# Experts as jobs of 256, 320 or 416 rows, with upper products of seven half-size products, on one Trainium2 core

## The reference

```python
def moe_swiglu(t, w_router, w1, w3, w2):
    logits = (t @ w_router).astype(jnp.float32)
    top_v, top_i = lax.top_k(logits, TOP_K)
    gates = jax.nn.softmax(top_v, axis=-1).astype(t.dtype)
    e_flat = top_i.reshape(-1)
    order = jnp.argsort(e_flat)
    tok = order // TOP_K
    xs = t[tok]
    sizes = jnp.bincount(e_flat, length=N_EXPERTS).astype(jnp.int32)
    h = jax.nn.silu(lax.ragged_dot(xs, w1, sizes)) * lax.ragged_dot(xs, w3, sizes)
    y = lax.ragged_dot(h, w2, sizes) * gates.reshape(-1)[order][:, None]
    return jnp.zeros_like(t).at[tok].add(y)
```

## Time and profile before

| | us |
|---|---|
| median of 3 runs | 9414.39 (9413.78 to 9432.35) |
| the profiled execution | 9423.43 |
| its span, first to last instruction | 9421.8 |
| TensorE busy | 8953.0 (95%) |
| VectorE busy | 2786.4 (30%) |
| ScalarE busy | 1255.4 (13%) |
| GpSimd (POOL) busy | 810.0 (9%) |

### The profile page before, as it was taken

How to read it: one execution, slowest core, us unless ns; L and a number is a source line. 1 busy time by engine, 2 the same in 40 slices (tenths; PEclk the granted TensorE clock), 3 DMA queues, 4 the chain that set the end, 5 groups by cost and what they waited for, 6 DMA issues and landing times. The chain is left out here.

```text
span 9421.8 us, 116793 instructions
## 1 busy us (share of the span) xinstructions
PE 8953.0 (95%) x45206; PEld 6543.9 (69%) x45207; DVE 2786.4 (30%) x5410; ACT 1255.4 (13%) x3193; POOL 810.0 (9%) x856
## 2 busy tenths in 40 slices
PE   9975999999999999889999999999999999999995
PEld 4454566557777767348777788777788777787774
DVE  2346455333343443541211211111111111111113
ACT  1134222220011110220000100000100000100002
POOL 0010000013343422010000000000000000000002
PEclk9986999999999999989999999999999999999997
DMA  5312000135555522233311211122211221211235
GB/s 223 134 48 88 12 6 6 71 132 198 190 209 194 207 86 83 84 135 107 115 67 67 92 42 53 53 93 80 91 67 67 76 71 67 92 53 67 89 107 196
DMA packets 498755, 922.04 MB, mean 98 GB/s; under 512 B 31404, under 2 KB 357084, under 8 KB 491632
## 3 DMA queue, kind: packets, MB, share of 16 engines
q1 hardware_dynamic: 426310, 667.60, 20.8%
q0 software_dynamic: 64320, 222.87, 6.1%
q10 hardware_dynamic: 7920, 28.84, 1.0%
HBM read 685.85 MB, written 231.23 MB: 97 GB/s over the span
## 5 line engine op out<-in xcount | busy, mean ns | idle before, releaser
L2610 PEld LDWEIGHTS ex_psH<-ex_xt,ex_w 128*128 128x128 f32 x23296 | 3331.9, 192 | 183.3 <-issue 183.3
L2610 PE MATMUL ex_psH<-ex_xt,ex_w 128*128 x23296 | 3385.6, 306 | 21.1 <-issue 18.1
L2620 PE MATMUL ex_psY<-ex_w,ex_a 128*128 128x512 f32 x2912 | 1309.9, 592 | 0.8 <-DVE ex_a L2769 0.8
L2769 DVE TENSOR_TENSOR ex_a<-ex_s,ex_psH 128x128 f32<-128x128 f32 (+1 forms) x728 | 237.3, 326 | 2958.3 <-ACT ex_s L2715 2958.3
L2620 PEld LDWEIGHTS ex_psY<-ex_w,ex_a 128*128 128x128 f32 x2912 | 535.3, 190 | 523.6 <-issue 520.6
L2776 DVE TENSOR_TENSOR ex_ya<-ex_psY,ex_ya 128x512 f32 (+2 forms) x676 | 571.5, 845 | 1046.5 <-PE ex_psY L2620 842.6
L2715 ACT ACTIVATE ex_s<-ex_psH 128x128 f32<-128x128 f32 (+1 forms) x728 | 224.2, 308 | 4532.0 <-PE ex_psH L2610 4531.9
L694 PE MATMUL de_ps<-de_w,de_big 128*128 128x512 f32 x1408 | 618.1, 596 | 24.8 <-DVE de_big L911 24.8
L694 PEld LDWEIGHTS de_ps<-de_w,de_big 128*128 128x128 f32 x1408 | 267.5, 191 | 350.1 <-issue 307.1
L259 PE MATMUL en_psO<-en_w,en_ht 128*128 128x512 f32 (+4 forms) x1152 | 473.4, 571 | 2.0 <-ACT en_ht L301 2.0
L2591 POOL DMA_DIRECT2D ys<-ex_ya x16 | 9.2, 573 | 5055.0 <-issue 5055.0
(11 more groups left out here) (387 smaller groups left out, 7054.2 us busy)
## 6 DMA issues: line engine op xcount, KB each, us to landing
ex_w<-in_o_w SPq DMA_DIRECT2D x336, 1024.0 KB, 7.7
de_wr<-in_e_w SPq DMA_DIRECT2D x88, 1024.0 KB, 5.3
xs<-de_zero POOLq DMA_DIRECT2D x130, 512.0 KB, 4.6
ys<-de_zero POOLq DMA_DIRECT2D x130, 512.0 KB, 5.4
en_ch<-in_w_mod SPq DMA_DIRECT2D x48, 1024.0 KB, 5.3
de_w<-in_e_w SPq DMA_DIRECT2D x44, 1024.0 KB, 5.1
ex_x<-xs ACTq DMA_DIRECT2D x55, 512.0 KB, 3.6
proj<-en_o POOLq DMA_DIRECT2D x18, 1008.0 KB, 4.2
```

Source lines behind the costliest of these rows:

```text
L2610: last = nc.tensor.matmul(psH[:, h, q * width:(q + 1) * width], W[:, s, k, h * P:(h + 1) * P], XT[:, k, bass.ds(at, width)], start=k == 0, ...
L2620: last = nc.tensor.matmul(psY[:, c], A[:, h, 0:P], W2[:, s, h, c * BANK:(c + 1) * BANK], start=h == 0, stop=h == HU - 1)
L2769: nc.vector.tensor_tensor(A[:, h, 0:width], S[:, h, 0:width], psH[:, h, width:2 * width], ALU.mult).then_inc(a_done, 1)
```

## The change

An expert is now cut into jobs of 2h rows, h being 128, 160 or 208. A table made on the host, `job_table`, gives for each number of 32-row units the cheapest set of jobs; on chip, VectorE picks for each expert the row of the table by its count, orders the jobs by size (all of 256 rows first, then 320, then 416) and writes a list with each job's first row, its expert and its half size. `experts` loops over the jobs of each size. The job is the outer loop now, and the chunks of 256 hidden columns the inner one, so every job streams its expert's 44 MB of weights again. YA holds one job and is double buffered; the stores to `ys` have moved from POOL to SyncE's queue. The upper products go by seven half-size products, `up` in the diff. Every job turns four tiles of 128 rows, for the next job, in its last two chunks (the `hooks`), and VectorE makes its four token sums (832 elements each) behind the last chunk's sums. The upper products are accumulated in PSUM banks 0 to 3, the down products in 4 to 6, and bank 7 takes the transposes. In `fourier` the old planning goes and the list's making comes in its place; `xs` and `ys` are six tiles of 128 rows longer.

```diff
+HALVES = (128, 160, 208)
+PS = m.psum("ps", [P, 8, BANK])
...
+def job_table():
+    sizes = [2 * h // UNIT for h in HALVES]
+    best = [(0.0,) + (0,) * NS]
+    for u in range(1, LEVELS):
+        options = []
+        for t, n in enumerate(sizes):
+            cost, *jobs = best[max(0, u - n)]
+            jobs[t] += 1
+            if sum(j * k for j, k in zip(jobs, sizes)) < LEVELS:
+                options.append((cost + n * UNIT + 6,) + tuple(jobs))
+        best.append(min(options))
+    return np.array([b[1:] for b in best], np.float32).T
...
 (fourier, VectorE: the list)
+            for e in range(NE):
+                last = nc.vector.scalar_tensor_tensor(PT[:, e], RI[:, 0:TABLE], U[:, e:e + 1], RI[:, TABLE:2 * TABLE], ALU.is_equal, ALU.mult)
+            settle(last)
+            settle(nc.vector.reduce_sum(SEG[:, :, 0:NE].rearrange("a t e -> a e t"), PT.rearrange("a e (t u) -> a e t u", t=NS), AXX))
...
+            for k in range(SEGS):
+                last = nc.vector.tensor_scalar(VQ[:, :, k], JOT, PRE[:, k:k + 1], DIF[:, k:k + 1], ALU.is_ge, ALU.mult)
+            settle(last)
+            settle(nc.vector.reduce_sum(JF[:, 0], VQ, AXX))
...
 (experts, SyncE: within a job)
+                    with sp.Fori(1, FC // 2) as q:
+                        for s in range(2):
+                            f = sp.snap((q * 2 + s).with_bounds(min_val=2, max_val=FC - 1))
+                            used(f - 2, 0)
+                            sp.dma_start(W1[:, s], pick(w1v, e, f)).then_inc(w1_in[s], 16)
+                            used(f - 2, 1)
+                            sp.dma_start(W3[:, s], pick(w3v, e, f)).then_inc(w3_in[s], 16)
+                            used(f - 2, 2)
+                            sp.dma_start(W2[:, s], pick(w2v, e, f)).then_inc(w2_in[s], 16)
...
 (TensorE)
+                        pe.wait_ge(comb["c22"], u + 1)
+                        product("p1", w, quarter(W, s, 0, 0), tokens(0, 0))
+                        pe.wait_ge(comb["c21"], u + 1)
+                        pe.wait_ge(sums["s2"], u + 1)
+                        pe.wait_ge(t_made, j + 1)
+                        product("p6", 2, SM[:, w, 1], token_sum(1))
+                        pe.wait_ge(comb["c12"], u + 1)
+                        product("p7", 3, SM[:, w, 0], token_sum(2))
+                        if hooks:
+                            half_turn(hooks[2 * w], j + 1)
+                        pe.wait_ge(comb["u2"], u + 1)
+                        product("p4", 2, quarter(W, s, 1, 1), token_sum(3))
+                        pe.wait_ge(kept, u + 1)
+                        product("p2", w, quarter(W, s, 0, 1), tokens(1, 0), start=False)
...
+                        product("p5", 1 - w, quarter(W, s, 1, 0), token_sum(0))
+                        if hooks:
+                            half_turn(hooks[2 * w + 1], j + 1)
+                        pe.wait_ge(comb["u3"], u + 1)
+                        pe.wait_ge(sums["s4"], u + 1)
+                        product("p3", 3, SM[:, w, 2], tokens(1, 1))
...
 (TensorE, down products: part o in bank 4 + o % 3)
+                            if o < 3:
+                                pe.wait_ge(y_added[t], first + 1)
+                            else:
+                                pe.wait_ge(y_added[t], first + (o - 1))
...
 (VectorE, a chunk)
+                        for w in range(2):
+                            combine(g, w, hooks)
+                        if hooks and hooks[-1] == 2 * TILES - 1:
+                            token_sums(dve.snap((j + 1).with_bounds(min_val=1, max_val=JOBS)), other)
...
+                        for o, (cols_n, r0, rows_n, c0, width, place) in enumerate(parts):
+                            dve.wait_ge(y_done[t], done + (o + 1))
+                            out, new = YA[:, bass.ds(y0 + place, width)], PS[:, 4 + o % 3, 0:width]
```

More of the change, by code:

```diff
@@ L2535, in plan @@
[L2535 to L2547, removed]
+        YA = m.sbuf("ya", [P, 2 * YW])
@@ L2563, in used @@
[L2563 to L2566, removed]
[L2568 to L2579 removed]
+            w1v = w1.rearrange("e (k p) (f n) -> e f p k n", p=P, n=FW)
@@ L2603, in _ @@
+            n, ahead = sized(pool, len(HALVES) - 1)
+            with pool.Fori(0, (n + ahead) * (FC // 2)) as q:
+                for s in range(2):
+                    for w in range(2):
+                        weight_sums(q * 4 + (2 * s + w), s, w, q)
         @block.tensor
         def _(pe):
+            pe.sem_inc(prod["p3"], 2)
             pe.wait_ge(const_in, 32)
-            def up(s, h, at, width):
-                for q, W in enumerate((W1, W3)):
-                    for k in range(KD):
-                        last = nc.tensor.matmul(psH[:, h, q * width:(q + 1) * width], W[:, s, k, h * P:(h + 1) * P], XT[:, k, bass.ds(at, width)],
-                                                start=k == 0, stop=k == KD - 1)
-                last.then_inc(up_done, 1)
@@ L2614, in down_first @@
-            def down_first(s, n, short):
-                pe.wait_ge(y_added, n + 1)
-                for h in range(HU):
-                    pe.wait_ge(a_done, n * HU + h + 1)
-                    for c in range(2):
-                        last = nc.tensor.matmul(psY[:, c], A[:, h, 0:P], W2[:, s, h, c * BANK:(c + 1) * BANK], start=h == 0, stop=h == HU - 1)
-                        if short and h == HU - 1 and c == 0:
-                            last.then_inc(y_done, 1)
-                last.then_inc(y_done, 1)
@@ L2694, in _ @@
         @block.scalar
         def _(act):
[L2697 to L2704 removed]
+            act.wait_ge(const_in, 32)
@@ L2752, in _, with take @@
         @block.vector
         def _(dve):
-            dve.sem_inc(y_added, 1)
+            dve.sem_inc(comb["c21"], 1)
+            dve.sem_inc(comb["c22"], 1)
+            dve.sem_inc(comb["c12"], 1)
+            dve.sem_inc(a_first, 1)
+            for t in range(len(HALVES)):
+                dve.sem_inc(y_added[t], 1)
             dve.wait_ge(const_in, 32)
-            def take(row, at):
-                dve.wait_ge(tr_done, row + 1)
+            def take(x, j, at):
+                t = x // 2
+                dve.wait_ge(tr_done, x + 1 if isinstance(j, int) else j * (2 * TILES) + x + 1)
@@ L2787, in _ @@
+            for x in range(0, 2 * TILES, 2):
+                take(x, 0, slice(0, 1))
+            token_sums(0, slice(0, 1))
             nc.vector.reciprocal(GK[:, 0], GG[:, 2]).then_inc(share, 1)
-            take(1, P)
             dve.wait_ge(share, 1)
```

636 lines of the change are left out of this document (374 added, 262 removed).

## The result

The changed kernel takes 9213.24 us (median of 4 runs, 9209.5 to 9213.99), the kernel before 9415.31 beside it (4 runs, 9413.78 to 9432.35): a ratio of 0.9781, 95% interval 0.9764 to 0.9798. The forecast was 9207.

The account below looks back on a forecast made before the run. TensorE's matmul stream was taken to bound the kernel. The stage at -230 us, the list +10 and the start +13 gave -207 on 9423.4, so 9216; the median, 9 lower, 9207 us, range 9155 to 9255.

Parts of the forecast that it names:

- the term for the chunks: Inside chunks: new waits priced at nothing, 5 us for weights and cover, hooks in last chunks included: 10 us.
- the slow clock: Behind each stop at a job's end, matmuls run slower: 0 to 3 us a stop, 1.5 taken, 21 us.
- the stream: TensorE's matmuls in all 14 jobs: chunks of 19.55, 24.26 and 31.19 us, 4685 us against 4989.
- the turns: Inside the stage, 14 jobs turn four tiles each, 56 at about 0.97 us: 54 us, 6 more than before.
- stops at the jobs' ends: TensorE, out of banks, waits for VectorE's additions behind stretched token sums: 4.35 us in each of 14 jobs, 61 us.
- two changes of size: Between jobs of different size, the last addition, two values loaded and some clock: 4 us each, 8 us.
- the list: Before the stage, making the job list takes 18 us in place of 6; +10 taken, as row landing may cover 2.
- the stage's start, to the first p1: Token loads, eight half turns one after the other and four token sums: 32 us against 19.1, +13.
- rival (a): Gaps between products from waits computed from registers, 0.12 us at each of 2744 products: 9536 us, slower than before; 7%.
- ScalarE's copies are of the same size and earlier: Inside a chunk, ScalarE's copies are like VectorE's operations and come sooner, so their waits were priced at nothing.
- Rival (d): Stops in narrow jobs' ordinary chunks, from POOL's sums meeting VectorE's multiplication or late c22: 0.3 us in 196 chunks, 9266; 12%.
- The estimate by the lock's full price: At a job's end, the first three token sums each wait out a whole POOL sum: 13 us more over 14 jobs, 9220.

Follow-up runs that it names:

- The experiment: The changed kernel with the last three token sums at a job's end put between VectorE's additions of the down products: 9137.86 us, ratio 0.97.
- the changed kernel's second profile: The changed kernel run again with no edit, as reference of its batch: 9219.58 us, ratio 0.9786.
- the one with the start edited: The changed kernel with the first job's eight half turns spread over four PSUM banks in place of bank 7 alone: 9201.83 us, ratio 0.9772.

## Why the prediction was right

The time was 6 us off, and the mechanism was right: TensorE's stream, with the stops where they were foreseen. That it came so near is in part luck. The table loads (21 us over the term for the chunks) and the slow clock (7) were missing, and the stream (23) and the turns (5) were too large by about as much; 7 us more come from stages that the change doesn't touch. The median was forecast 9 us under the profiled execution and lay level with it. In the profiled execution (9212.9 us, forecast 9216), step by step:

| step | forecast | measured |
|---|---|---|
| stream of the 14 jobs | 4685 | 4662: chunks of 19.37 (as without the loads), 24.14 and 31.19 us |
| turns | 54 | 49: 112 half turns of 0.44 |
| waits inside chunks, hooks | 10 | 31, all of it table loads |
| stops at the jobs' ends | 61 | 57.1 |
| slow clock behind them | 21 | 28 |
| two changes of size | 8 | 11: 3.30 us each, and 1.6 and 2.9 at the slow clock |
| the first p6 and its wait | none | 5: 2.22 us, and slow records |
| the stage against before | -230 | -222 |
| the list | +10 | +5 |
| the stage's start, to the first p1 | +13 | +13 (31.9 us) |
| the end | 0 | -2 |
| stages before the list | none | -7 |
| `finish` | none | +2 |

- **The stream** was right in kind: nothing but columns and rows sets it, and rival (a) is dead, as products of 8 records start 0.893 us apart in a job of 256 rows, 0.1116 us a record, and the records of before, with a wait at every 32, were 0.1133 apart. The size was 0.12 to 0.18 us a chunk too large for 256 and 320 rows.
- **"ScalarE's copies are of the same size and earlier"** is the step that failed. The copies' size was right and their time was not: before a chunk's first copy stood a load of 1.28 us, in 48 of the 56 chunks of the jobs of 256 rows. No row has a load, and the forecast took that for granted in a new loop. The trace of before does have 16 in this stage, each before a SiLU:

```profile
L2715 ACT ACT_TABLE_LOAD x16 | 20.5, 1283 | 14.5 <-issue 14.3
```

There they cost TensorE next to nothing (its waits for the products of the SiLU are 0.8 us in all), but they were the sign that this stage can load. The copy had 1.79 us of cover (p6 and p7), the load took 1.28 of them, and what stayed was less than the copy and u2 need. Rival (d) gave 0.3 us in 196 chunks (59 us) to another cause; it was 0.65 us in 47 (31 us). POOL's sums beside VectorE's multiplication, and c22, cost nothing: with the loads gone no product waits in a chunk (0.0 us for p4 and p5; the waits left in the other groups are those of the stage's start and the changes of size).
- **The stop at a job's end** was right in place, cause and size: 4.30 us against 4.35, from `dense`'s stretched operations. Its cause is shown by taking POOL's reads away. The estimate by the lock's full price (13 us more over 14 jobs) was too high. Counted from start to start a stop is 4.46 us (from 4530.36 to 4539.97, less 12 records of 0.429).
- **The clock behind a stop** was the right mechanism, 2.2 us in place of 1.5. The experiment's busy time gives it, not the idle time.
- **The changes of size** show that the length of a stop alone doesn't set its price. Both took 3.30 us, and behind both the first records ran at half speed here. Behind the same stop of 3.30 us they ran at full speed in the changed kernel's second profile (second change) and without POOL's reads (first change). The first changes here and without POOL's reads, then the second changes here and in the second profile:

```profile
5415.28 2.50 PE L2752 MATMUL ex_ps<-ex_xt,ex_w 128*128 x8 [3.30 <-issue]
5394.49 1.35 PE L2757 MATMUL ex_ps<-ex_xt,ex_w 128*128 x8 [3.30 <-issue]
...
8204.76 3.13 PE L2752 MATMUL ex_ps<-ex_xt,ex_w 128*128 x8 [3.30 <-issue]
8214.96 1.67 PE L2752 MATMUL ex_ps<-ex_xt,ex_w 128*128 x8 [3.31 <-issue]
```

- **The list** hid more than the 2 us allowed: 11 us more planning moved the stage by 5. That the landing of the scattered rows held the stage before is not shown; the DMA share is 0.00 from 4214 us on, and the stage began at 4220.15.
- **The start** came out as forecast to the first p1. But p6 waits for the token sums, which are made after the last half turn, and p1 and p6 ran slow (2.07 and 3.55 us where 1.06 and 1.95 are usual): 5 us that the forecast hadn't.
- The 7 us of earlier stages are not the change's: the changed kernel profiled again has its first turn at 4236.15, 7 us later than this execution, and the one with the start edited 14 us later. What sets that spread was not looked into. Of the stage's terms some 4 us stay unassigned; about 2 of them are the part of 13 stops that the idle column leaves out (4.46 against 4.29).

## What to carry to other kernels

Where a loop on ScalarE uses two functions, look for table loads in the trace of *that* loop: they don't follow from the order of operations one reads, and one dummy call ahead of the loop may take all of them out. Where an engine has two kinds of work due at a boundary, and another engine holds buffers for one of them, interleave them in the order in which they are missed: here that is worth 82 us, a third of it TensorE's clock. And price a stop at what the same records cost behind it, as well as at its idle time.

## What the runs showed of the hardware

- Granted clock after a stop: 0.50 (1.2 GHz) behind the stop of 4.3 us at 4540 us, with 28 us over the 13 such stops; 1.00 behind one of 1.1 us. Behind the stops of 3.3 us at the changes of size the records show both: 8 records of 160 columns in 2.50 us in one run and in 1.35 in another, of 208 columns in 3.13 and in 1.67.
- VectorE's operations with two SBUF inputs of 832 columns: 1.02 us alone, 2.08 long and 2.00 apart beside POOL's sums; POOL's 1.27 become 1.93.
- A load of ScalarE's table is 1.28 us; before the copy in these chunks, where 0.51 us of cover are left, it costs TensorE 0.65 us where the idle time shown is 0.33 or 0.42.
